# Sums of squares of query and key heads: one f32 product or two rounded ones, one head behind or two, in a two-layer decoder step

## The reference

```python
def attn_project(h, w_in, g_q, g_k, g_kidx):
    q, k, v, qi, ki, wi = jnp.split(h @ w_in, ATTN_SPLITS, axis=-1)
    q = rms_norm(q.reshape(B, T, N_HEADS, HEAD_DIM), g_q)   # 8 heads of 128
    k = rms_norm(k.reshape(B, T, N_HEADS, HEAD_DIM), g_k)   # 8 heads of 128
    ...
def index_scores(qi, ki, wi):
    logits = jnp.einsum('bthd,bsd->bths', qi, ki) * IDX_DIM ** -0.5
    return jnp.einsum('bth,bths->bts', w, jax.nn.relu(logits))
# then: top-64 (prompt) and top-65 (sample) keys of the scores, softmax over them, values
```

## Time and profile before

| what | us |
|---|---|
| median of 3 runs | 1511.49 (1511.29 to 1511.58) |
| the profiled execution, its own time | 1510.78 |
| span of its trace | 1509.1 |
| PE / DVE / ACT / POOL busy | 1495.8 / 1214.4 / 991.3 / 164.2 |
| granted TensorE clock, mean | 0.999 |

### The profile page before, as it was taken

How to read it: one execution, slowest core, us unless ns; L and a number is a source line. 1 busy time by engine, 2 the same in 40 slices (tenths; PEclk the granted TensorE clock), 3 DMA queues, 4 the chain that set the end, 5 groups by cost and what they waited for, 6 DMA issues and landing times.

```text
span 1509.1 us, 21654 instructions
## 1 busy us (share of the span) xinstructions
PE 1495.8 (99%) x8215; PEld 1276.8 (85%) x8215; DVE 1214.4 (80%) x1106; ACT 991.3 (66%) x955; POOL 164.2 (11%) x162
## 2 busy tenths in 40 slices
PE   9999999999999999999999999999999999999998
PEld 7887789999997987888888888888888888888887
DVE  4689787666545869888888888889889888888887
ACT  4444665444445577777777777777777777777775
POOL 3554000000000036401001001001000000000100
PEclk9999999999999999999999999999999999999999
DMA  7651983345554359999999999999999999999990
GB/s 220 232 226 56 365 304 134 126 144 203 206 190 163 119 190 374 365 393 382 394 395 382 393 396 383 393 394 383 393 392 360 397 376 379 376 396 370 376 359 32
DMA packets 198855, 456.92 MB, mean 303 GB/s; under 512 B 12020, under 2 KB 15134, under 8 KB 198794
## 3 DMA queue, kind: packets, MB, share of 16 engines
q1 hardware_dynamic: 190802, 439.34, 78.5%
q0 software_dynamic: 4336, 13.15, 3.0%
q10 hardware_dynamic: 3656, 3.60, 0.8%
HBM read 444.04 MB, written 12.03 MB: 302 GB/s over the span
## 4 chain that ended last, share of the span: by engine, by line
PE 93%; DVE 4%; ACT 1%; issue 1%; DMA 0%; ACTq 0%; DVEq 0%
PE bank L2071 22%; PE bank L2591 13%; PE bank L2593 13%; PE bank L2592 13%; PE bank L2605 7%; PE bank L2607 7%; PE bank L2606 7%; PE bank L2615 2%; PE bank L2363 1%; PE bank L2264 1%; PE bank L2058 1%; DVE rt L1611 1%; PE bank L2159 1%; PE bank L2276 1%; DVE sc L1592 0%
## 5 line engine op out<-in xcount | busy, mean ns | idle before, releaser
L1856 DVE TENSOR_TENSOR wql<-ring,wqh 128x2048 fp32r<-128x2048 f32 x335 | 766.8, 2291 | 107.7 <-ACT wqh L1000 106.7
L1000 ACT ACTIVATE wqh<-ring 128x2048 fp32r<-128x2048 f32 x334 | 641.5, 1921 | 230.2 <-PE bank L2593 147.8
L2591 PE MATMUL bank<-wqh,xgh 128*128 128x512 f32 x892 | 353.6, 396 | 0.3 <-DVE wql L1856 0.3
L2592 PE MATMUL bank<-wql,xgh 128*128 128x512 f32 x896 | 349.1, 390 | 0.0
L2593 PE MATMUL bank<-wqh,xgl 128*128 128x512 f32 x892 | 348.0, 390 | 0.0
L2593 PEld LDWEIGHTS bank<-wqh,xgl 128*128 128x128 f32 x892 | 167.5, 188 | 35.9
L2591 PEld LDWEIGHTS bank<-wqh,xgh 128*128 128x128 f32 x892 | 167.5, 188 | 34.3 <-DVE wql L1856 1.1
L2592 PEld LDWEIGHTS bank<-wql,xgh 128*128 128x128 f32 x896 | 168.4, 188 | 32.9
L1000 ACT ACTIVATE wd<-ring 128x1024 fp32r<-128x1024 f32 x90 | 95.1, 1059 | 133.6 <-PE bank L2071 131.3
L2605 PE MATMUL bank<-wqh,heTh 128*128 128x512 f32 x440 | 171.4, 389 | 0.0
L2607 PE MATMUL bank<-wqh,heTl 128*128 128x512 f32 x440 | 171.2, 389 | 0.0
(11 more groups left out here) (457 smaller groups left out, 2047.8 us busy)
## 6 DMA issues: line engine op xcount, KB each, us to landing
ring<-in_moe_w_gate SPq DMA_DIRECT2D x56, 2048.0 KB, 13.8
ring<-in_moe_w_up SPq DMA_DIRECT2D x56, 2048.0 KB, 13.9
ring<-in_moe_w_down SPq DMA_DIRECT2D x56, 2048.0 KB, 13.5
ring<-in_attn_w_in SPq DMA_DIRECT2D x7, 2048.0 KB, 12.7
ring<-in_ffn_w_gate SPq DMA_DIRECT2D x5, 2048.0 KB, 11.3
ring<-in_ffn_w_up SPq DMA_DIRECT2D x5, 2048.0 KB, 7.9
ring<-in_cache_k SPq DMA_DIRECT2D x16, 512.0 KB, 7.0
ring<-in_cache_v SPq DMA_DIRECT2D x16, 512.0 KB, 6.1
```

The source lines that it names most:

```text
L1000: return nc.scalar.activation(dst, src, ACT.Copy)
L1856: return v.tensor_tensor(dst, src, head.bitcast(F32), ALU.subtract)
L2591: mm(bank, xgh[:, k, :], w_h[:, part], start=(k == 0), stop=False)
L2592: mm(bank, xgh[:, k, :], w_l[:, part], start=False, stop=False)
```

## The change

- The matrix of ones becomes a rounded one (`ones_r`). The squares of a head are split: ACT copies `sq2` into a rounded `square_head`, POOL subtracts that from `sq2` into `square_tail` (new semaphores `sqh_ok`, `sql_ok`), and `head_ssq` is two fp32r products that add up in one bank. The three-deep buffers `sqs` lie where `qz` is later.
- `head_ssq(n - 1)` becomes `head_ssq(n - LAG)` with LAG = 2. The last two sums come after the first two quarters of the value projection (`between`).
- ACT takes the root of head n-2 in turn n, and its square of head n waits for the tail of head n-2. POOL takes `low_square(n)` ahead of `tail_of(n + 4)` for n = 0 to 15, and masks the prompt scores after quarter 16 (n = 12) instead of before it.
- The indexer's pieces `kio`, `iss`, `isel`, `is` go to group B, between the sums `qkn`; `vs` stays in A.
- DVE takes its first step of `choosing` at head 2 instead of 4, and the sample scores at head 1 instead of 3.

```diff
@@ order of the banks
-        if n:
-            B.add(("qkn", n - 1), "act")
+        if n >= LAG:
+            B.add(("qkn", n - LAG), "act")
         if n == 1:
-            A.add("kio", "act")
-            A.add(("iss", 0), "act")
+            B.add("kio", "act")
+            B.add(("iss", 0), "act")
         elif n == 2:
-            A.add(("iss", 1), "act")
+            B.add(("iss", 1), "act")
         elif n == 3:
-            A.add("isel", "dve")
+            B.add("isel", "dve")
         if n in SCORES:
-            A.add(("is", SCORES[n]), "act")
+            B.add(("is", SCORES[n]), "act")
...
@@ POOL
+        def low_square(n):
+            if n >= SQ:
+                pool.wait_ge(*B.full(("qkn", n - SQ)))
+            pool.wait_ge(sqh_ok, n + 1)
+            nc.gpsimd.tensor_tensor(square_tail(n), sq2[:, n % 2, :], square_head(n).bitcast(F32), ALU.subtract)\
+              .then_inc(sql_ok, 1)
...
+        for n in range(WRING):
             tail_of(n)
...
+        for n in range(16):
+            low_square(n)
+            if n == VQ0 - WRING:
+                pool.wait_ge(*A.full(("vs", 1)))
+            tail_of(n + WRING)
+            if n == 12:
+                pool.wait_ge(score_ok, 2)
...
@@ ACT
-        for n in range(17):
+        for n in range(16 + LAG):
             if n < 16:
                 act.wait_ge(*A.full(("qk", n)))
                 if n >= 2:
-                    act.wait_ge(*B.full(("qkn", n - 2)))
+                    act.wait_ge(sql_ok, n - 1)
                 nc.scalar.activation(sq2[:, n % 2, :], A.ap(("qk", n))[:, 0:T], ACT.Square).then_inc(qsq, 1)
+                if n >= SQ:
+                    act.wait_ge(*B.full(("qkn", n - SQ)))
+                act.wait_ge(qsq, n + 1)
+                copy(square_head(n), sq2[:, n % 2, :]).then_inc(sqh_ok, 1)
                 heads_before(n + 1 + WRING)
-            if n >= 1:
-                j = n - 1
+            if n >= LAG:
+                j = n - LAG
...
@@ DVE
-            if n == 3:
+            if n == 3 - LAG:
                 take_sample_scores()
...
-            for _ in range(0 if n < 4 else 1 if n < 9 else 2):
+            for _ in range(0 if n < 4 - LAG else 1 if n < 9 else 2):
                 next(choosing, None)
@@ PE
+                if between is not None and q < LAG:
+                    between(16 - LAG + q)
...
         def head_ssq(n):
             B.room(pe, ("qkn", n))
-            pe.wait_ge(qsq, n + 1)
-            mm(B.ap(("qkn", n))[:, 0:T], ones[:], sq2[:, n % 2, :], start=True, stop=True).then_inc(b_full, 1)
+            pe.wait_ge(sqh_ok, n + 1)
+            mm(B.ap(("qkn", n))[:, 0:T], ones_r[:], square_head(n), start=True, stop=False)
+            pe.wait_ge(sql_ok, n + 1)
+            mm(B.ap(("qkn", n))[:, 0:T], ones_r[:], square_tail(n), start=False, stop=True).then_inc(b_full, 1)
...
-            if n:
-                head_ssq(n - 1)
+            if n >= LAG:
+                head_ssq(n - LAG)
             indexer(n)
-        head_ssq(15)
         for half in range(2):
-            project_tokens_split("v", half, VQ0 + QU * half, hE_r)
+            project_tokens_split("v", half, VQ0 + QU * half, hE_r, between=head_ssq if half == 0 else None)
```

More of the change, by code:

```diff
@@ L54 @@
 V_AT = 11
+SQ = 3
+LAG = 2
 QU = 4
@@ L137, in build @@
     ident = sb("ident", [P, P])
-    ones = sb("ones", [P, P])
+    ones_r = sb("ones", [P, P], F32R)
+    ones = ones_r[:].bitcast(F32)
     under = ExitStack()
@@ L217, in build @@
     tok = sb("tok", [P, 3, D], stack=under)
+    with ExitStack() as norms:
+        sqs = sb("sqs", [P, 2 * SQ, T], F32R, stack=norms)
     qz = sb("qz", [P, H * NSEQ, NS], stack=under)
@@ L408, in build @@
             A.add(("vs", 1), "dve")
-    B.add(("qkn", 15), "act")
+    for n in range(16 - LAG, 16):
+        B.add(("qkn", n), "act")
     for half in range(2):
@@ L690, in _ @@
             if n == RING + 1:
-                sp.wait_ge(*A.full(("is", 5)))
+                sp.wait_ge(*B.full(("is", 5)))
                 sp.wait_ge(*A.freed("wrep"))
-                sp.wait_ge(*A.freed("isel"))
+                sp.wait_ge(*B.freed("isel"))
             if name == ("vp", 3):
@@ L815, in tail_of @@
               .then_inc(p_tail, 1)
-        for n in range(VQ0):
-            tail_of(n)
[L819 to L824, removed]
+        def low_square(n):
[5 more added lines that the diff above has]
+        for n in range(WRING):
+            tail_of(n)
+        for n in range(16):
[5 more added lines that the diff above has]
+                pool.wait_ge(score_ok, 2)
+                select(sc0[:], ALU.is_ge, NEG, 0, [[-1, P]], 1)
+                select(sc1[:], ALU.is_ge, NEG, P, [[-1, NP]], 1).then_inc(masked, 1)
+        for n in range(VQ0 + WRING, F0):
             tail_of(n)
+        pool.wait_ge(*B.full(("qkn", 15)))
         pool.wait_ge(*A.freed(("kipt", 3)))
@@ L1093, in take_indexer @@
                 act.wait_ge(h_tail, KD)
-                act.wait_ge(*A.full(("is", g)))
-                nc.scalar.activation(rl[:, g, :], A.ap(("is", g))[:], ACT.Relu, scale=ID ** -0.5).then_inc(a_act, 1)
+                act.wait_ge(*B.full(("is", g)))
+                nc.scalar.activation(rl[:, g, :], B.ap(("is", g))[:], ACT.Relu, scale=ID ** -0.5).then_inc(b_act, 1)
             elif n == V_AT:
@@ L1549, in take_sample_scores @@
         def take_sample_scores():
-            dve.wait_ge(*A.full("isel"))
-            v.tensor_copy(scs[:], A.ap("isel")[0:NS, 0:WS]).then_inc(a_dve, 1)
-            dve.wait_ge(*A.freed("isel"))
+            dve.wait_ge(*B.full("isel"))
+            v.tensor_copy(scs[:], B.ap("isel")[0:NS, 0:WS]).then_inc(b_dve, 1)
+            dve.wait_ge(*B.freed("isel"))
             link(v.tensor_tensor(scs[:, PAST:WS], scs[:, PAST:WS], vmask[:], ALU.mult))
@@ L2096, in to_tokens, with project_tokens_split @@
             last.then_inc(a_full, 1)
-        def project_tokens_split(name, half, n0, tails, seen=None):
+        def project_tokens_split(name, half, n0, tails, seen=None, between=None):
             for m in range(3):
@@ L2204, in indexer @@
                     last = mm(rows[:, PAST:WS], q, kiT[:, NP + TS * b:NP + TS * b + TS], start=True, stop=True)
[L2205 removed]
+                last.then_inc(b_full, 1)
             if n == 3:
[L2207 removed]
+                B.room(pe, "isel")
                 pe.wait_ge(*A.freed("wrep"))
                 for g in range(2):
[L2210 to L2212 removed]
+                    pe.wait_ge(*B.freed(("iss", g)))
+                    last = mm(B.ap("isel")[0:NS, 0:WS], selw[:, g, :], rls[:, g, :], start=(g == 0), stop=(g == 1))
+                last.then_inc(b_full, 1)
             if n in SCORES:
                 g = SCORES[n]
[L2215 removed]
+                B.room(pe, ("is", g))
                 i = 0 if g < 2 else 1
```

41 lines of the change are left out of this document (20 added, 21 removed).

## The result

The kernel after took 1518.64 us (median of 20 runs) beside 1512.67 for the kernel before in the same session. The ratio on record is 1.0024 (95% 1.0013 to 1.0034); the two medians alone would give 1.0039, since the times fall into groups. Forecast were 1513.7, in a range that ended at 1515.6.

What follows compares the result with a forecast made beforehand. DVE's last run of heads, not PE's 93% share, was taken to bound the stretch. Head 10 at 104.3 less 99.86, 1.93 and 0.25 gave +2.2 on 1510.78, 1513.0; plus 0.7 for the median, 1513.7, range 1511.6 to 1515.6.

Steps and rivals of the forecast that it cites:

- The product and the bank order: Head sums on PE fall from 0.48 to 0.27 us; PE stalls 1.2 us once, in turn 3, before `is` 0.
- POOL beside DVE: POOL's subtractions hold DVE's two-input score steps at heads 7 to 9, so head 10 starts at 104.3.
- the case that I gave 103.5: Nothing holds DVE: head 10 starts 2.33 us after ACT's square of head 12 at 101.2.
- DVE's work left: At head 10 DVE is two steps ahead, 1.93 us, and loses 0.25 idle; its end moves +2.2 us.
- PE after the loop: PE waits 4.3 us for head 12's bank before the values; DVE still comes last, at 143.6.
- The sum: Whole program: 1510.78 + 2.2 = 1513.0 us for a profiled execution; 0.7 more for the runs' median, 1513.7.
- the last one: From profiled execution to median: the runs' median lies 0.7 us above, so 1513.0 becomes 1513.7.
- The rival in which the clock falls: PE's wait from 111.7 to 116.0 takes the clock to 1.2 GHz: 1.6 us on top, 1515.3; chance 0.2.
- Held steps: DVE score steps beside POOL's tails, in the sum at heads 7 to 9; rival of one more, 1516.1, chance 0.08.

Runs made afterwards that it cites:

- e1: The kernel after with one bank moved: the prompt scores `is` 0 back in bank group A; median 1512.49 us, ratio to before 1.0004.
- e4: The kernel after with its sum as one f32 product over the rounded squares alone, tails left out; median 1515.66 us, ratio to before 1.0020.
- g1: The kernel before with ten spare 128x512 products in the router and gather stretch; median 1511.44 us, ratio to before 0.9993.
- g2: The kernel after with ten spare 128x512 products in the router and gather stretch; median 1513.38 us, ratio to before 1.0007.
- e6: The kernel after with LAG = 1, `is` 0 in group A and two steps of `choosing` from head 8 on; median 1514.82 us, ratio to before 1.0011.
- e7: e6 with each 128x1024 tail subtraction of POOL issued as four instructions; median 1517.61 us, ratio to before 1.0020.
- e2: The kernel after with LAG = 1 instead of 2, so one head behind; median 1516.16 us, ratio to before 1.0019.
- e3: The kernel after with LAG = 1 and all banks of the indexer in group A; median 1517.45 us, ratio to before 1.0033.

## Why the prediction was right or wrong

*The product and the bank order: right.* Forecast 0.27 a sum (of which the saving ahead of head 12 is 2.6, where I wrote 2.7) and a stall of 1.2 for ACT's root; measured 0.13 + 0.13 and 1.11. Head 10's square was forecast at 90.5 and came at 90.38, head 12's at 101.2 and came at 101.20.

*POOL beside DVE: right in kind, one step too many.* Head 7 at 89.4 (89.31), held until 95.3 (95.10). POOL's low square takes 0.81 to 0.93, not 0.70. By my own terms POOL had 0.4 us free a turn (3.47 less 0.70 and 2.39), not the 0.9 that I wrote; measured it was about 0.2. The last hold, of head 9's steps by the low square of head 12, did not happen: the low square began at 102.29, when the steps were nearly through (102.46). So head 10 started at 103.59, not 104.3, set by the root as in the case that I gave 103.5.

*DVE's work left: right.* 103.59 - 99.86 - 1.93 - 0.25 = 1.55, and the first copy is 1.55 later. e1 and e4 moved head 10 by -1.2 and +2.0 and the copy by as much.

*PE after the loop: wrong in form.* I had one wait of 4.3 us for head 12's bank. Six places back from head 14 in group A is head 10, and from head 15 head 11, in before as in after. In before these banks were free in time; now that DVE comes to head 10 only at 103.59, both heads had to wait, 0.82 and 0.62, and then the values 1.43: 2.87 in all. They began at 115.64 (forecast 116.0). The prediction went through the rooms of the values and not those of the last heads. Nothing at the end hung on it; DVE still came last, by 0.65.

*The sum: right for an undisturbed execution.* +2.2 forecast, +2.0 measured. Of these 1.6 are at the turned keys and at the router (542.70 against 541.09); the other 0.4 I did not trace.

*The step that failed is the last one, from the profiled execution to the median; it put the time outside the range.* The sum adds 0.7 for the runs' median over the profiled execution, because the three runs shown of before lay within 0.3 us. That treated the clock as a constant. It is not: the median lies 5.7 us above the executions of after that kept their clock (1518.64 less 1512.9), and for before 1.8 (1512.67 less 1510.9). With 18 of after's 31 executions at a fallen clock, its median lies among the fallen ones. The rival in which the clock falls had a loss of 1.6 us, too small, and the wrong place and cause: it was to follow the wait from 111.7 us. There PE was busy 9.77 of 12 us and the clock stayed at 1.00. The wait of 4.3 us that it needed never came in one piece, so no run tests what such a wait would do. The Trainium skill (TensorE: Matmul & The Clock Gate, A second HAM failure mode: psum-queue depth-cycling) also tells, of a kernel with bf16 products of 512 columns, that many small pauses between groups of matmuls can make the clock go back and forth. This case's rows agree in part: the clock falls behind small waits, once and not back and forth, and with spare products there (g1, g2) it stays. Had I looked for such waits, those of before at 541 to 548 would have given me a rival with the right place. Its size and its chance they would not have given: before's windows there show 1.00, and why after falls more often is open.

*Held steps.* The Trainium skill (GPSIMD Engine Reference, Key points) says that GpSimd's SBUF interfaces are shared with VectorE, with contention for instructions with two SBUF inputs. The traces agree and give its price, which that page doesn't: up to the rest of the POOL instruction (6.85 us for four steps in e6, 3.70 in e7), and none for the reciprocal, at 1.95 throughout. I took it into the sum; in e2, e3 and e6 I left it out of the expectations, and all three have held steps ahead of head 10. In e2 and e6 the stall ahead of `iss` 0 comes on top.

## What to carry to other kernels

A saving on the engine with the largest share counts only as far as the engine that ends the stretch starts sooner: here 2 us of cheaper sums did arrive, but one early bank (1.2 us, e1) and, by the rows, waiting one head longer cost more. When the order of operations over banks changes, go through the room of every later user, for the old ones too: three kernels here (e2, e6, e7) stalled 1.9 us or more on a bank freed in the same turn. Before forecasting a median within a few microseconds, look at the granted clock of several executions and at each stretch where TensorE does small products between small waits; a few spare products there lowered after's median by 5 us.

## What the runs showed of the hardware that I had not expected

- The clock of a kernel at 99% PE fell to 1.2 GHz behind a stretch whose longest wait was 0.51 us, and cost that execution 6.8 us of full clock. A mean clock of 0.996 or less came in 18 of 31 executions of after and 27 of 128 of before, and in none of 46 with spare products in that stretch.
- In after nothing of the kind came at waits of 0.6 to 1.4 us among dense 128x288 products at 103 to 116 us. In e7 the clock did fall behind a wait of 2.01 us; in e6 it stayed behind one of 1.91.
- The clock also fell some 10 to 20 us into the program, to 0.50 of full speed over those 10 us in e1, and not in every execution of a kernel.
- Cutting each POOL subtraction of 2.39 us into four of 0.75 brought four DVE steps beside them from 6.85 to 3.70 us (2.0 alone), at 0.6 us of POOL for each subtraction.
